# Differential attention: scores two units ahead on 64-row halves, one maximum per unit, squares on ScalarE

## The reference

```python
q = rms(q) * q_g ; k = rms(k) * k_g          # 8 heads, 2 maps, 64 wide; rope on the latent tokens
lam = exp(sum(lq1 * lk1)) - exp(sum(lq2 * lk2)) + lam_init
def attend(qb, kb, vb):                      # v: 8 heads, 128 wide
    s = einsum('bqhmd,bkhmd->bmhqk', qb, kb) * 64 ** -0.5
    p = softmax(s, axis=-1)                  # for each of the two maps m
    a = p[:, 0] - lam * p[:, 1]
    o = einsum('bhqk,bkhe->bqhe', a, vb)
    return rms(o) * sub_g * (1.0 - lam_init)
```

## Time and profile before

| | us |
|---|---|
| median of three runs | 3372.44 |
| lowest and highest run | 3370.17, 3373.92 |
| the profiled execution | 3368.4 |
| its span | 3366.5 |
| mean granted TensorE clock | 0.947 of full speed |
| TensorE busy | 2702.9 (80%) |
| VectorE busy | 2065.6 (61%) |
| ScalarE busy | 676.0 (20%) |

### The profile page before, as it was taken

One profiled execution on the slowest core, in us unless ns is written; L12 is line 12 of the kernel. 1 busy time (PEld: TensorE's weight loads), 2 busy tenths in 40 slices (PEclk: granted clock), 3 DMA queues, 4 the chain that ended last, 5 costly groups with the idle time before them and its releaser, 6 DMA issues. The chain is left out here.

```text
span 3366.5 us, 31270 instructions
## 1 busy us (share of the span) xinstructions
PE 2702.9 (80%) x9228; PEld 1337.6 (40%) x9228; DVE 2065.6 (61%) x4825; ACT 676.0 (20%) x1667; POOL 1086.5 (32%) x927
## 2 busy tenths in 40 slices
PE   5898699998679998877777777776996688877776
PEld 1342488888244443222222222322443444422222
DVE  1334233333437677888888888886236277788887
ACT  1115223332021111111111111112024121111111
POOL 0001423230104344444444444442000044444553
PEclk9899799999889999999999999998999799999999
DMA  8336100000148999999999999996300399999998
GB/s 330 106 113 251 46 1 1 1 1 2 74 182 342 395 376 389 420 420 420 414 420 421 421 416 420 419 421 252 151 3 0 125 419 420 420 416 419 420 419 334
DMA packets 135749, 927.55 MB, mean 276 GB/s; under 512 B 17100, under 2 KB 18124, under 8 KB 31716
## 3 DMA queue, kind: packets, MB, share of 16 engines
q0 software_dynamic: 111744, 805.46, 58.1%
q1 hardware_dynamic: 23912, 120.88, 9.4%
HBM read 925.13 MB, written 1.15 MB: 275 GB/s over the span
## 5 line engine op out<-in xcount | busy, mean ns | idle before, releaser
L1343 PE MATMUL psum<-ring,diag 128*128 128x512 f32 x3072 | 1486.2, 623 | 371.8 <-DVE diag L1432 370.0
L1240 POOL DMA_INDIRECT ring<-in_uv,experts x768 | 921.6, 1200 | 1368.3 <-PE psum L1343 1010.6
L1454 DVE CUSTOM_DVE_ANT_0 ring<-ring,hcur 128x1024 f32<-128x1024 f32 x768 | 941.4, 1226 | 258.2 <-DMA ring<-in_uv,experts 237.5
L1343 PEld LDWEIGHTS psum<-ring,diag 128*128 128x128 f32 x3072 | 558.6, 194 | 1274.7 <-DVE diag L1432 795.9
L1274 ACT ACTIVATE gel<-dots 128x1 f32<-128x1 f32 x768 | 143.5, 201 | 1325.4 <-DVE dots L1454 1324.8
L1432 DVE TENSOR_SCALAR diag<-ident,gel,wcur 128x128 f32<-128x128 f32 x768 | 256.3, 344 | 80.6 <-ACT gel L1274 80.6
L991 DVE COPY_PREDICATED T<-level,psum 128x512 f32<-128x512 uint32 x80 | 58.8, 735 | 184.2 <-PE psum L802 184.2
L339 PE MATMUL psum<-zT,wring 128*128 128x512 f32 x368 | 161.7, 600 | 6.6 <-DMA wring<-in_w_in 6.6
L1323 PE MATMUL psum<-hT,w_q 128*128 128x512 f32 (+3 forms) x512 | 163.1, 473 | 0.7 <-DMA w_q<-in_w_q 0.7
L1516 PE MATMUL psum<-wring,zT 128*128 128x512 f32 x320 | 140.0, 601 | 11.0 <-DMA wring<-in_w_qkv 11.0
L1323 PEld LDWEIGHTS psum<-hT,w_q 128*128 128x128 f32 x512 | 94.5, 190 | 67.8 <-issue 57.9
(11 more groups left out here) (316 smaller groups left out, 2574.0 us busy)
## 6 DMA issues: line engine op xcount, KB each, us to landing
wring<-in_w_mod SPq DMA_DIRECT2D x12, 2048.0 KB, 12.6
wmod<-in_w_mod SPq DMA_DIRECT2D x24, 1024.0 KB, 8.9
w_q<-in_w_q SPq DMA_DIRECT2D x32, 512.0 KB, 7.7
ring<-in_uv,experts POOLq DMA_INDIRECT x768, 10.8
wring<-in_w_qkv SPq DMA_DIRECT2D x6, 2048.0 KB, 8.7
wring<-in_w_in SPq DMA_DIRECT2D x23, 512.0 KB, 3.7
bc<-modulation_rows SPq DMA_DIRECT2D x14, 512.0 KB, 5.0
w<-in_w_out SPq DMA_DIRECT2D x8, 512.0 KB, 6.3
```

The lines of the kernel that those rows point to most:

```text
L1240: nc.gpsimd.indirect_dma_start(ring[:, s % RING], None, uv, bass.IndirectOffsetOnAxis(ap=experts[:, n, j:j + 1], axis=0)).then_inc(row_in[ ...
L1343: m = nc.tensor.matmul(ps[:, c], diag[:, j % DIAGS], ring[:, j % RING, D + 512 * c:D + 512 * c + 512], start=(first and j == 0), stop=(las ...
L1454: nc.vector.tensor_tensor_reduce(u, u, hcur[:], 1.0, 0.0, ALU.mult, ALU.add, dots[:, j:j + 1]).then_inc(dot_done, 1)
```

## The change

It does the following in `attention`, and nothing elsewhere:

- qT holds both maps of a head on the 128 rows, without zeros. Each score matmul takes 64 rows of qT and of kT. POOL's memset is gone, and q is copied out as k is.
- Scores are computed two units ahead of A, in three pairs of banks (`DEEP = 3`). To make room, the turned A has one bank (`TURN = 6`) and the values have one (`OUT = 7`) instead of two each.
- One maximum over both maps' banks gives two numbers per row, and one instruction negates both.
- ScalarE squares the values of a unit straight from PSUM and sums them (L1671 of the changed kernel). `copy_out` comes behind it and multiplies by sub_g.
- The end no longer squares and sums on DVE; it multiplies by the reciprocal root in two halves and releases each half by itself.
- On DVE the maxima of u+2 stand behind A(u) and `copy_out(u-1)`; before, the maxima of u+1 stood ahead of A(u).

```diff
-                    if u >= 2:
-                        pe.wait_ge(exp_done, 2 * (u - 1))
+                    if u >= DEEP:
+                        pe.wait_ge(exp_done, 2 * (u - DEEP + 1))
                     for m in range(2):
-                        nc.tensor.matmul(ps[:, 2 * (u % 2) + m], qT[:, m, h, t * P:(t + 1) * P], kT[:, h],
-                                         start=True, stop=True).then_inc(s_mm, 1)
+                        rows = slice(HD * m, HD * m + HD)
+                        i = nc.tensor.matmul(ps[:, 2 * (u % DEEP) + m], qT[rows, h, t * P:(t + 1) * P], kT[rows, h], start=True, stop=True)
+                    i.then_inc(s_mm, 1)
...
+                    if u >= 1:
+                        pe.wait_ge(o_done, u)
+                    for k in range(TILES):
+                        m = nc.tensor.matmul(ps[:, OUT, 0:P], aT[:, u % 2, k], v[:, k, h * P:(h + 1) * P],
...
                 scores(0)
+                scores(1)
                 for u in range(NU):
-                    if u + 1 < NU:
-                        scores(u + 1)
+                    if u + 2 < NU:
+                        scores(u + 2)
...
-                    if g < 4:
-                        act.wait_ge(q_zero, 1)
-                        for m in range(2):
-                            rows = slice(HD * m, HD * m + HD)
-                            nc.scalar.activation(qT[rows, m, 2 * g:2 * g + 2].rearrange("p h t -> p (h t)"),
-                                                 ps[rows, g % 8], ACT.Copy).then_inc(tr_done, 1)
-                    else:
-                        nc.scalar.activation(kT[:, g - 4], ps[:, g % 8], ACT.Copy).then_inc(tr_done, 1)
+                    dst = qT[:, 2 * g:2 * g + 2].rearrange("p h t -> p (h t)") if g < 4 else kT[:, g - 4]
+                    nc.scalar.activation(dst, ps[:, g % 8], ACT.Copy).then_inc(tr_done, 1)
...
+                def squares(u):
+                    act.wait_ge(pv_mm, u + 1)
+                    if u >= 2:
+                        act.wait_ge(sq_done, u - 1)
+                    nc.scalar.activation(sq[:, u % 2], ps[:, OUT, 0:P], ACT.Square, accum_out=ss[:, u % 2, u // 2:u // 2 + 1]).then_inc(sq_done, 1)
...
                     if u + 1 < NU:
                         softmax(u + 1)
+                    if u >= 1:
+                        squares(u - 1)
                     act.wait_ge(at_mm, u + 1)
...
+                    nm = nmax[:, u % 2]
+                    dve.wait_ge(s_mm, u + 1)
+                    step(nc.vector.tensor_reduce(nm, ps[:, pair(u)], AX, ALU.max))
+                    nc.vector.tensor_scalar(nm, nm, -SCALE, None, ALU.mult).then_inc(max_done, 1)
 
                 def copy_out(u):
-                    dve.wait_ge(pv_mm, u + 1)
-                    nc.vector.tensor_copy(o[:, u % 2, u // 2], ps[:, 6 + u % 2, 0:P]).then_inc(o_done, 1)
+                    dve.wait_ge(sq_done, u + 1)
+                    tt(o[:, u % 2, u // 2], ps[:, OUT, 0:P], sub_g[:], ALU.mult).then_inc(o_done, 1)
...
-                    if u >= 2:
-                        copy_out(u - 2)
-                copy_out(NU - 2)
+                    if u >= 1:
+                        copy_out(u - 1)
+                    if u + 2 < NU:
+                        maxima(u + 2)
                 copy_out(NU - 1)
-                dve.wait_ge(o_done, NU)
-                flat = lambda x: x[:].rearrange("p t h d -> p (t h) d")
-                step(tt(sq[:], o[:], o[:], ALU.mult))
-                step(nc.vector.tensor_reduce(ss[:], flat(sq), AX, ALU.add))
...
-                step(tt(flat(o), flat(o), ss[:].unsqueeze(2).broadcast_to([P, 2 * HEADS, P]), ALU.mult))
-                tt(flat(o), flat(o), sub_g[:].unsqueeze(1).broadcast_to([P, 2 * HEADS, P]), ALU.mult).then_inc(on_done, 1)
+                dve.wait_ge(o_done, NU)
+                for t in range(2):
+                    tt(o[:, t], o[:, t], ss[:, t].unsqueeze(2).broadcast_to([P, HEADS, P]), ALU.mult).then_inc(on_done, 1)
```

More of the change, by code:

```diff
@@ L1602, in scores, with values @@
                     h, t = u // 2, u % 2
-                    if u >= 2:
-                        pe.wait_ge(exp_done, 2 * (u - 1))
+                    if u >= DEEP:
+                        pe.wait_ge(exp_done, 2 * (u - DEEP + 1))
                     for m in range(2):
-                        nc.tensor.matmul(ps[:, 2 * (u % 2) + m], qT[:, m, h, t * P:(t + 1) * P], kT[:, h],
-                                         start=True, stop=True).then_inc(s_mm, 1)
+                        rows = slice(HD * m, HD * m + HD)
+                        i = nc.tensor.matmul(ps[:, 2 * (u % DEEP) + m], qT[rows, h, t * P:(t + 1) * P], kT[rows, h], start=True, stop=True)
+                    i.then_inc(s_mm, 1)
+                def values(u):
+                    h = u // 2
+                    pe.wait_ge(at_done, u + 1)
+                    if u >= 1:
+                        pe.wait_ge(o_done, u)
+                    for k in range(TILES):
+                        m = nc.tensor.matmul(ps[:, OUT, 0:P], aT[:, u % 2, k], v[:, k, h * P:(h + 1) * P],
+                                             start=(k == 0), stop=(k == TILES - 1))
+                    m.then_inc(pv_mm, 1)
                 for g in range(12):
                     if g >= 8:
-                        pe.wait_ge(tr_done, 2 * (g - 7))
+                        pe.wait_ge(tr_done, g - 7)
                     for c in range(4):
@@ L1615, in _ @@
                     m.then_inc(tr_mm, 1)
[L1616 to L1619, removed]
-                    if u >= 2:
[L1621 to L1625, removed]
+                pe.wait_ge(tr_done, 12)
                 scores(0)
+                scores(1)
                 for u in range(NU):
-                    if u + 1 < NU:
-                        scores(u + 1)
+                    if u + 2 < NU:
+                        scores(u + 2)
                     if u >= 1:
@@ L1675, in _ @@
                         act.wait_ge(pv_mm, u - 1)
-                    nc.scalar.activation(aT[:, u % 2].rearrange("p k t -> p (k t)"), ps[:, 4 + u % 2], ACT.Copy).then_inc(at_done, 1)
+                    nc.scalar.activation(aT[:, u % 2].rearrange("p k t -> p (k t)"), ps[:, TURN], ACT.Copy).then_inc(at_done, 1)
+                squares(NU - 1)
                 act.wait_ge(var_done, 1)
@@ L1701, in maxima @@
                 def maxima(u):
[L1702 to L1705, removed]
-                        nc.vector.tensor_scalar(nm, nm, -SCALE, None, ALU.mult).then_inc(max_done, 1)
+                    nm = nmax[:, u % 2]
+                    dve.wait_ge(s_mm, u + 1)
+                    step(nc.vector.tensor_reduce(nm, ps[:, pair(u)], AX, ALU.max))
+                    nc.vector.tensor_scalar(nm, nm, -SCALE, None, ALU.mult).then_inc(max_done, 1)
                 def copy_out(u):
-                    dve.wait_ge(pv_mm, u + 1)
-                    nc.vector.tensor_copy(o[:, u % 2, u // 2], ps[:, 6 + u % 2, 0:P]).then_inc(o_done, 1)
+                    dve.wait_ge(sq_done, u + 1)
+                    tt(o[:, u % 2, u // 2], ps[:, OUT, 0:P], sub_g[:], ALU.mult).then_inc(o_done, 1)
                 maxima(0)
+                maxima(1)
                 for u in range(NU):
                     b = u % 2
-                    if u + 1 < NU:
-                        maxima(u + 1)
                     dve.wait_ge(exp_done, 2 * u + 2)
```

30 lines of the change are left out of this document (14 added, 16 removed).

## The result

| | before | changed |
|---|---|---|
| median us (lowest to highest) | 3371.69 (3370.17 to 3373.92, 4 runs) | 3340.53 (3337.99 to 3344.02, 4 runs) |
| ratio, with its 95% interval | 1 | 0.9906 [0.9894, 0.9918] |
| the profiled execution's span | 3366.5 | 3341.1 |
| attention phase, first DMA to the next phase's first | 113.36 | 82.07 |
| mean granted clock | 0.947 | 0.951 |

The changed kernel is 31 us faster; 33 were forecast, and 3339. A second timing, beside the last experiments, gave 35 us and 0.9897 [0.9880, 0.9913]. The two spans differ by only 25.4 us. The rest arose ahead of the change: the attention phase of the changed kernel's profile begins at 2512.13 where that of before begins at 2505.70, although the code up to there is the same. Behind the phase both take 747 us (747.4 before, 746.9 changed).

A forecast was written before the change was run, and what follows sets the result against it. Attention was taken to be bound by a loop through TensorE, VectorE and ScalarE, none full. Savings 2.95 + 0.5 + 23.7 + 6.8 = 34, less 1 for clock, 33, took the median 3372.44 to 3339 us; range 3331 to 3348.

The forecast's parts named there:

- Bound and cover: Attention phase: its three-engine loop sets the time, and no later transfer hides what the phase gives back.
- Head: Start of attention: four full-height q copies save 2.95 us; first score to first full A pass saves 0.5.
- Halves side by side: Scores on TensorE: two 64-row halves overlap, 0.86 instead of 1.72 us per unit, plus 0.1; each switch 0.09.
- Rival 1: Scores: halves do not overlap at 512 columns, 3.73 a unit, 3344 us; chance 0.15 together with a colder clock.
- The loop: Attention units: turn, scores, values, Square and copy out in series, two units in 6.76 us, 3.38 a unit.
- two exponentials from 1.19, and is free at 2.95: this ends last: ScalarE in the loop: counted from the turn's start, its exponentials end at 2.95 us, after the values at 2.79.
- The rival of full-height scores: Experiment's forecast by the predicted loop: with scores over 128 rows, 3.73 us a unit and a phase of 89.
- VectorE: VectorE's work per unit with one maximum (1.22 us, 1.33 with gap and negation): 3.20 us, the least a unit takes.
- Loop in all: First A pass to read of the last values: 76.68 us becomes 52.95, 23.7 less; 1 taken off for half clock.
- Tail: Last values to first output transpose: 10.60 us becomes 3.8, 6.8 less, with a 1.28 table load exposed.
- Clock: TensorE half clock: 1 us allowed; two or three further stretches 3342, warm head 3337, whole loop 3353; mild end within 0.77.
- The shorter idling of TensorE speaks against: Argument against the whole loop running at half clock, which would give 4.4 us a unit and 3353 us.

The follow-up runs named there:

- full-height scores: Changed kernel with q copied and scores computed over all 128 rows as before the change: 3345.30 us.
- later turn: Changed kernel with three more transposes, their results overwritten, ahead of each turn of A on TensorE: 3336.22 us.
- maximum first: Changed kernel with VectorE's maximum of u+2 placed ahead of the copy out of u-1: 3333.42 us.
- the version with the early load: Changed kernel with the maximum of u+2 ahead of the copy out of u-1, and a dead Sqrt ahead of the last Square: 3331.27 us.
- one unit ahead: Changed kernel with scores and maxima only one unit ahead, as before the change; halves, single maximum and Squares stay: 3374.39 us.
- the halves alone: Kernel before with only the 64-row score halves added (q copied whole, no zeros): 3387.47 us.
- the changed kernel's second profile: Changed kernel unaltered, run again for comparison on one chip: 3338.08 us, phase 82.06.

## Why the prediction was right, step by step

- **Bound and cover.** Right: the phase's 31.3 us came through to the end, and what lies behind it kept its 747.
- **Head.** Forecast 2.95 and 0.5; measured 2.82 and 0.87. Both maps were ready 2.19 after the first score, as one map was before. The halves carry all of this: with full-height scores the first A pass comes 21.37 us after the first DMA, 20.99 in the kernel before and 17.30 in the changed one.
- **Halves side by side.** Right at 512 columns: four instructions in 1.13, the values 1.65 behind the turn where 1.64 was added up. The switch costs 0.10 (0.59 against 0.49). The Trainium skill, in TensorEngine Tiling (Array Packing), Key Properties, says that a change of mode drains TensorE; whatever it does here, the trace shows 0.10 us for it and no stall of a matmul's length. Rival 1 falls. But what the overlap is worth was wrong: in the loop as it is, 0.02 us a unit. I had set 5 us on it. It paid 1.6 us at the head, which rival 1 left out.
- **The loop.** The number was near (3.38, measured 3.46), the mechanism wrong, so the nearness is luck. The step that failed is "two exponentials from 1.19, and is free at 2.95: this ends last". I let the exponentials start when ScalarE was free and did not ask when their maximum was done. That maximum stands on VectorE behind the copy out that waits for the Square, so it comes late: the exponentials began 1.92 behind the turn. What made the number come out all the same is a second error, the other way: back to back they take 0.67, not 0.88, as the accumulator read overlaps. One is 0.73 too early, the other 0.42 too long, and the Square with its copy out came 0.08 quicker: 0.23 are left on two units, and VectorE's shorter work takes 0.08 of them. The rival of full-height scores and the later turn show the difference, the one by 3.48 instead of 3.73, the other by 3.45 instead of 3.62.
- **VectorE.** Forecast 3.20 as its least; 3.10 with the maximum first. The single maximum was sized from a maximum at 512 columns and a multiply at 2048, two different operations; 1.22 was right all the same.
- **Loop in all.** From the first A pass to the read of the last values 76.68 was 55.98: 20.7 less, where 23.7 less 1 for the clock stood. Most of what is missing is the half clock at the third A pass, 5.93 - 3.46 = 2.5, of which I had allowed 1; the slower unit adds 13 x 0.08 = 1.0, and a first unit of 2.91 gives 0.5 back. The kernel before had such a stretch too. With head and tail each some 0.2 and 0.1 better than forecast, the phase is 31.3 shorter where 33 stood.
- **Tail.** Forecast 6.8, measured 6.89, the exposed load of 1.28 included. The Trainium skill, in ScalarE: Activation LUTs, What ACT_TABLE_LOAD costs, adds a drain of 1.38 to the 1.28 of each load. Here it is not to be seen: the load starts 0.02 after the Square's accumulator read has ended, and the root follows the load's start by 1.29, as the early Sqrt does in the version with the early load.
- **Clock.** Under-sized: 1 us was allowed, one profile lost 2.5 at the second unit and the other 2.7 in the tail. And it was too lightly taken as a rival. "The shorter idling of TensorE speaks against" held only since the change lengthens the lead and shortens the matmuls together. Each half of that pair by itself was not what it looked: one unit ahead, or the halves alone, and the loop is slower than before the change.

What stays open: which of the stages ahead of attention let the phase begin up to 10 us earlier or later was not looked for, nor why the changed kernel's second profile fell to half clock at 2571.8 while its loop was still running.

## What to carry to other kernels

When an engine's operation is placed by adding up what lies ahead of it on that engine, ask for each of its operands too when it is made, and what the maker waited for: an in-order queue hides a loop in its order, and swapping two independent instructions there (the maximum and the copy out) was worth 4.2 us in the loop, where halving the time of TensorE's scores was worth 0.2. Read the pitch of back-to-back instructions where nothing gates them, not from busy times added up. Where TensorE is not the bound, making its work shorter can lower its clock and slow the loop: test such a part alone only with the idle time in view.

## What was not expected of the hardware

Filling TensorE's waits with transposes nobody reads took the loop of the halves alone from 86.3 to 74.2 us, with the granted clock over the same 59.5 us of span rising from 0.76 to 1.00. An exponential of 512 columns with its accumulator read repeats every 0.67 us although the two rows add up to 0.88. And four float32 instructions on two 64-row halves, 512 columns each, end 1.13 us after the first began, where two at full height would take 1.02 by their pitch and last duration (0.43 and 0.59).
